# A fused attention and DeltaNet layer on one core: two head steps moved in a hand-written slot schedule

## What is computed

```python
bqkv = short_conv(bqkv, conv_w)                 # 4 taps back in time, then SiLU
g = -exp(a_log) * softplus(balpha + dt_bias);  beta = sigmoid(bbeta)
q = l2_normalize(q) * dk ** -0.5;  k = l2_normalize(k)
decay = exp(where(causal, g[i] - g[j], -inf))   # g summed up over the tokens
lower = where(strict, (k * beta) @ k.T * decay, 0)
tmat  = inverse(eye + lower)                    # unit lower triangular
...                                             # products with tmat, q and the state
o = rms_norm(o, dn_norm_gain) * silu(bz)
merged = sigmoid(gate_a) * (ya @ w_branch_a) + sigmoid(gate_b) * (yb @ w_branch_b)
out = rms_norm(x + merged @ w_out)
```

## Time and profile before

| what | value |
|---|---|
| median of 3 runs | 838.61 us (836.59 to 840.05) |
| the profiled execution, its own time | 838.09 us |
| its span, first to last instruction | 836.4 us |
| mean granted TensorE clock | 0.996 of full speed |
| busy: PE, PEld, DVE, ACT, POOL | 811.0, 665.5, 484.0, 411.0, 140.3 us |
| moved by DMA | 142.15 MB, 170 GB/s over the span |

### The profile page before, as it was taken

The page is one execution under the profiler, slowest core; times in us unless marked ns, Lnnn a source line. Parts: engine busy times, 40 slices in busy tenths (PEclk is TensorE's granted clock), DMA queues, the critical chain, the costliest instruction groups (busy, mean ns, idle before and its releaser), DMA issues.

```text
span 836.4 us, 12563 instructions
## 1 busy us (share of the span) xinstructions
PE 811.0 (97%) x3859; PEld 665.5 (80%) x3859; DVE 484.0 (58%) x794; ACT 411.0 (49%) x641; POOL 140.3 (17%) x222
## 2 busy tenths in 40 slices
PE   8899999999999999999999999999999999999996
PEld 7788877878787888778877878787788778888874
DVE  4676448545754664576448555754664466775562
ACT  4564545544544555454545544544555464444441
POOL 9112112110211021102112110211031100001120
PEclk9999999999999999999999999999999999999999
DMA  8855564565556455655565565556455565678652
GB/s 210 230 150 175 137 188 141 167 176 150 176 150 167 135 176 150 176 150 176 146 180 151 150 175 150 176 150 176 126 177 149 176 196 183 188 220 295 194 160 100
DMA packets 179207, 142.15 MB, mean 170 GB/s; under 512 B 10880, under 2 KB 144240, under 8 KB 179056
## 3 DMA queue, kind: packets, MB, share of 16 engines
q1 hardware_dynamic: 179184, 141.85, 58.4%
HBM read 139.72 MB, written 2.10 MB: 170 GB/s over the span
## 4 chain that ended last, share of the span: by engine, by line
PE 43%; issue 36%; POOL 8%; DVE 6%; ACT 3%; SPq 2%; DMA 1%; POOLq 0%; DVEq 0%; ACTq 0%
PE pj L498 12%; PE pj L496 12%; PE pj L497 12%; POOL xo L429 4%; POOL mt L427 3%; ACT w_hi L783 1%; PE dn_ps L551 1%; DVE w_lo L1008 1%; DVE conv L1118 1%; DVE decay L1105 1%; ACT L848 1%; SPq L268 1%; SPq L251 1%; POOL kn L423 1%; DVE conv L1115 1%
## 5 line engine op out<-in xcount | busy, mean ns | idle before, releaser
L1008 DVE TENSOR_TENSOR w_lo<-w_raw,w_hi 128x1024 fp32r<-128x1024 f32 x251 | 312.1, 1249 | 182.6 <-ACT w_hi L783 181.9
L496 PE MATMUL pj<-w_hi,xt_hi 128*128 128x512 f32 x860 | 357.1, 415 | 2.9 <-DVE w_lo L1008 2.8
L498 PE MATMUL pj<-w_hi,xt_lo 128*128 128x512 f32 x860 | 338.7, 394 | 0.0
L783 ACT ACTIVATE w_hi<-w_raw 128x1024 fp32r<-128x1024 f32 x251 | 264.6, 1059 | 149.7 <-PE pj L498 133.2
L497 PE MATMUL pj<-w_lo,xt_hi 128*128 128x512 f32 x860 | 336.4, 391 | 0.0
L498 PEld LDWEIGHTS pj<-w_hi,xt_lo 128*128 128x128 f32 x860 | 161.7, 188 | 36.6
L496 PEld LDWEIGHTS pj<-w_hi,xt_hi 128*128 128x128 f32 x860 | 162.6, 189 | 33.0 <-issue 3.5
L497 PEld LDWEIGHTS pj<-w_lo,xt_hi 128*128 128x128 f32 x860 | 162.9, 189 | 27.6
L429 POOL TENSOR_TENSOR xo<-v,own 128x128 f32<-128x128 f32 x48 | 44.6, 930 | 233.5 <-DVE v L1172 231.7
L872 ACT ACTIVATE ysb<-dn_ps 128x128 f32<-128x128 f32 x48 | 13.2, 276 | 63.0 <-PE dn_ps L568 63.0
L1172 DVE TENSOR_TENSOR v<-v,dn_ps 128x128 f32<-128x128 f32 x48 | 13.8, 287 | 45.5 <-PE dn_ps L573 44.6
(11 more groups left out here) (259 smaller groups left out, 784.0 us busy)
## 6 DMA issues: line engine op xcount, KB each, us to landing
w_raw<-in_w_in_dram SPq DMA_DIRECT2D x384, 256.0 KB, 3.1
w_raw<-in_w_out_dram SPq DMA_DIRECT2D x64, 256.0 KB, 3.7
w_raw<-in_w_branch_a_dram SPq DMA_DIRECT2D x32, 256.0 KB, 3.4
w_raw<-in_w_branch_b_dram SPq DMA_DIRECT2D x32, 256.0 KB, 3.6
gate<-in_x_dram SPq DMA_DIRECT2D x8, 256.0 KB, 5.5
gate<-in_x_dram SPq DMA_DIRECT2D x4, 512.0 KB, 7.5
gate<-in_final_norm_gain_dram SPq DMA_DIRECT2D x1, 1024.0 KB, 9.1
out_dram<-gate SPq DMA_DIRECT2D x1, 768.0 KB, 3.6
```

The lines of the kernel that those rows point to most:

```text
L496: pe.matmul(bank[:, t, :], hi[:, k, tok], w_hi[:, slot, cs], start=(k == 0), stop=False)
L498: mm = pe.matmul(bank[:, t, :], lo[:, k, tok], w_hi[:, slot, cs], start=False, stop=(k == kt_all - 1))
L783: act.activation(w_hi[:, slot, :], w_raw[:, slot, :], ACT.Copy).then_inc(hi_ready, 1)
L1008: dve.tensor_tensor(w_lo[:, slot, :], w_raw[:, slot, :], w_hi[:, slot, :].bitcast(F32), ALU.subtract).then_inc(lo_ready, 1)
```

## The change

It moves pieces between slots and cuts one wait in two.

- `S_Y0`, `S_R1`, `S_Y1`, `S_O` and `S_YT` stand two slots later (55, 57, 59, 61, 65).
- PE's L576 waits for the first mask of `xf` alone; the wait for the second stands ahead of L583.
- `S_DEC` is 16 in heads 1 to 7 and stays 20 in the first head. DVE's five decay blocks go with it, ahead of the convolution; the last two taps keep slot 20 (`S_CONV`). ACT's `Exp` follows in slot 17.
- ACT's SiLU goes from slot 23 to slot 22, where it stands ahead of the slot's weight copy.
- ACT's copy of the next head to `dn_nat` gets a wait for `o_squared`.

```diff
-S_TURN, S_DEC, S_KK = 18, 20, 24
+S_DEC, S_TURN, S_CONV, S_SILU, S_KK = 16, 18, 20, 22, 24
+S_DEC_FIRST = 20
-S_Y0, S_R1, S_Y1, S_O, S_YT = 53, 55, 57, 59, 63
+S_Y0, S_R1, S_Y1, S_O, S_YT = 55, 57, 59, 61, 65
...
-                if s == S_DEC:
+                if s == (S_DEC_FIRST if first else S_DEC):
                     pe.wait_ge(hs_ready, h + 1)
...
                 if s == S_Y0:
-                    pe.wait_ge(xf_ready, T * h + T)
+                    pe.wait_ge(xf_ready, T * h + 1)
...
                 if s == S_Y1:
                     pe.wait_ge(r1_ready, h + 1)
+                    pe.wait_ge(xf_ready, T * h + T)
...
                         act.wait_ge(dn_z_ready, h)
+                        act.wait_ge(o_squared, T * h)
...
-                if s == S_DEC + 1:
+                if s == (S_DEC_FIRST if first else S_DEC) + 1:
                     act.wait_ge(dsub_ready, 5 * (h + 1))
                     act.activation(decay[:, :, :], decay[:, :, :], ACT.Exp).then_inc(dexp_ready, 1)
-                if s == S_KK - 1:
+                if s == S_SILU:
                     act.wait_ge(conv_step, 12 * h + 12)
...
-                if s in (S_TURN, S_DEC):
+                if s == (S_DEC_FIRST if first else S_DEC):
+                    dve.wait_ge(dec_done, h + 1)
+                    if not first:
+                        dve.wait_ge(kk_ready, 3 * h)
...
+                                                 op0=ALU.subtract, op1=ALU.add).then_inc(dsub_ready, 1)
...
+                                          0.0, ALU.add, ALU.min).then_inc(dsub_ready, 1)
+                if s in (S_TURN, S_CONV):
...
                     for back in ((0, 1) if s == S_TURN else (2, 3)):
-                        if back == 2:
...
```

More of the change, by code:

```diff
@@ L1088, in dn_step @@
             def dn_step(s, h, first=False):
-                if s in (S_TURN, S_DEC):
+                if s == (S_DEC_FIRST if first else S_DEC):
+                    dve.wait_ge(dec_done, h + 1)
+                    if not first:
+                        dve.wait_ge(kk_ready, 3 * h)
+                    e1 = E[:, P:2 * P]
+                    e1_flip = E[:, 2 * P - 1:P - 1:-1]
+                    for block, t, e, mask in ((D00, 0, E[:, 0:P], later), (D11, 1, e1, later_flip),
+                                              (D11R, 1, e1_flip, earlier)):
+                        dve.scalar_tensor_tensor(out=decay[:, block, :], in0=e,
+                                                 scalar=hs[:, C_CUM + t:C_CUM + t + 1], in1=mask[:, :],
+                                                 op0=ALU.subtract, op1=ALU.add).then_inc(dsub_ready, 1)
+                    for block, e in ((D01, e1), (D01R, e1_flip)):
+                        dve.tensor_scalar(decay[:, block, :], e, hs[:, C_REST:C_REST + 1],
+                                          0.0, ALU.add, ALU.min).then_inc(dsub_ready, 1)
+                if s in (S_TURN, S_CONV):
                     if s == S_TURN:
```

## The result

The changed kernel takes **824.84 us** (median of 4 runs, 823.2 to 826.69), the kernel before 838.39 us in the same comparison (836.59 to 840.05). The ratio is 0.9843, 95% interval 0.9825 to 0.986. The profiled execution took 824.77 us, with a span of 823.1 us against 836.4. The forecast was 825.4 us, and 824.9 us for the profiled execution.

A forecast was written before the change was run, and what follows sets the result against it. PE's own work and the holes in it bound the kernel. Terms 8.9 + 5.7 + 0.8 - 2.2 = 13.2 us took the profiled 838.09 to 824.9; the median forecast was 825.4 us, range 821.5 to 831.0.

The forecast's parts named there:

- L577, two slots later: PE's wait for POOL's `xf`, 1.11 us a head, goes with the two-slot shift: gain 8.9 us.
- L552, `convs` in time: PE's wait for ACT's `convs` goes with the SiLU ahead of the weight copy: gain 5.7 us.
- L593 behind the loop: PE's single wait for `yb` behind the loop goes: gain 0.8 us, an estimate between 0 and 0.8.
- L539, new wait: PE's transposes of slot 18 wait for DVE's `yb_lo`, 0.32 us a head in 7 heads: -2.2 us.
- Reading the holes from start to start: On PE's timeline, a wait's loss exceeds its idle time: 1.11 us against 0.84, 0.72 against 0.47.
- The other count of a table load: On ACT, 1.38 us drain plus 1.28 us load; first head keeps its wait, sum 12.2 in place of 13.2.
- For PE that is worth about 0: Decay rows in slot 16 end DVE's convolution earlier, sparing 0.9 us, but gain PE about 0.
- a row of L538 that names `yb_lo`: Expected sign in PE's waits: 7 times, 0.1 us or less idle, some 0.3 to 0.5 us each on PEld.
- The bigger wait: Rival at PE's transposes of slot 18: each head gives back 1.45 us instead of 0.32, 833.3 us; chance 0.13.
- `hs` was copied 2.1 us before L547: Check at `S_DEC`: 2.0 us to spare; slower rival, `hs` late holds PE, 845.6 us at 5.2 late; chance 0.03.
- L497 waited for `w_lo`: Rival that the holes move: PE's weight stream can't follow, the gain is gone, 838 +- 4; chance 0.06.

The follow-up runs named there:

- Run 1: Kernel before with only the five later steps shifted by two slots, plus the cut wait: 828.03 us against 838.19.
- run 10: Changed kernel, but L577 waits for both masks again: 824.71 us against 837.14 for the kernel before.
- run 4: Kernel before, every step in its old slot, with only the wait cut so that L577 waits for the first mask: 834.48 us against 837.89.
- runs 2 and 3: Kernel before with the cut wait plus one move: the SiLU in slot 22 (829.66 us), or the decay rows in slot 16 (829.37 us), against 838.19.
- run 11: Changed kernel with the five steps one slot later than before in place of two: 822.48 us against 837.89 for the kernel before.
- run 5: Kernel before with only the SiLU moved to slot 22, the full wait for both masks kept: 833.0 us against 837.89.
- runs 3 and 7: First: kernel before with the decay rows' move and the cut wait, 829.37 us. Second: changed kernel with the SiLU back in slot 23, 825.43 us.
- run 6: Changed kernel without the decay rows' move, slot 20 in every head: 821.9 us against 838.19 for the kernel before.
- run 8: Changed kernel with DVE's split of slot 16 put in slot 17 behind `yb_lo`, in heads 1 to 7: 822.67 us against 837.14.
- run 9: Changed kernel with three more decay-like DVE instructions ahead of the five blocks in heads 1 to 7: 830.32 us against 837.14.
- Run 12: Kernel before, with DVE's split of slot 4 waiting for both of POOL's masks in heads 1 to 7: 831.3 us against 837.85.

## Why the prediction was right

The terms of the sum, each beside what the trace of the changed kernel shows:

| term | predicted | measured |
|---|---|---|
| L577, two slots later | 8.9 | 8 x (1.48 - 0.38) = 8.8 |
| L552, `convs` in time | 5.7 | 7 x 0.72 + 0.63 = 5.7 |
| L593 behind the loop | 0.8 | wait row gone; 1.14 to 0.37 us, 0.8 |
| L539, new wait | -2.2 | -7 x (1.14 - 0.80) = -2.4 |
| sum | 13.2 | 12.9; the span lost 13.3 |

The last two numbers differ in part by PE's wait at the start for the DMA of `x` (L482, now L483): 1.1 us before, 0.5 after. It is in no term of the sum and lies between 0.3 and 1.5 us in these traces. That 13.2 comes as near as 0.1 to 13.3 is so far luck; that each term is right to 0.2 us is not.

- **Reading the holes from start to start** carried the forecast. The idle times in the earlier trace rows add up to 10.9 us. The trace gave back 15.3, and then lost 2.4.
- **The shift.** Run 1, the shift without the other moves, gained 10.2 us where its two terms say 9.7. That the cut wait adds nothing to it is shown by run 10. What I had not priced is the cut without the shift: it is worth 3.4 us (run 4), which is why runs 2 and 3 came out below what I expected. And one slot would have been enough for the mask (run 11).
- **The SiLU.** The table load did begin ahead of the convolution's end, by 3.4 us. "This move alone takes away nearly all of the loss" holds: 4.9 us in run 5, where the trace leaves 0.06 us a head of the wait. The other count of a table load, by which the first head would have kept its wait (a sum of 12.2), is answered by the first head: the load ran from 55.08 to 56.36, the convolution ended at 56.62, the SiLU began at 56.65, and L552 started 0.23 us behind the last large matmul, as without a wait.
- **The decay rows.** "For PE that is worth about 0" holds beside the SiLU's move. What I had not said is that either of the two clears the wait of `convs` by itself (runs 3 and 7). So in the change one of them is spare: the rows' move in all heads, or the SiLU's in all but the first. Without the rows' move the time is 821.9 (run 6), and L539's steps are 2.1 us shorter in all. The prediction had both numbers, -2.2 for the new wait and about 0 for the rows, and didn't set them against each other.
- **The new wait.** DVE's blocks started 0.74 us behind L547, the split 1.30 later, `yb_lo` 1.13 later, all as forecast. PE started 3.73 us behind L547, not 3.64, since it needed 0.14 us behind `yb_lo`'s end, not 0.06; so it was 0.30 us late, not 0.21. The first product then cost 0.04 more, not 0.11 (and the two waits that I took this from say 0.10). Two small errors cancelled: 0.34 a head for 0.32. That DVE's order makes this wait is shown by runs 6, 8 and 11, which take it away but for 0.00 to 0.06 us in three different ways, and by run 9, which adds 0.78 us to its cause and finds no slack.
- **What I said of the views** was partly wrong. I expected a row of L538 that names `yb_lo`. PE's waits have none after the change, and PEld's put it down to issue, 0.5 us each. In runs 7 and 10, with the same order in DVE, PE's waits name it for one of the seven, 0.2 us.
- **A slip** in the range: 823.2 less 2.0 is 821.2, where I wrote 821.5. The result lies far from it.
- **The rivals.** The bigger wait didn't come: DVE's split of slot 14 ended 1.2 us before the blocks began, by DVE's idle time ahead of them. `hs` was copied 2.1 us before L547, against 2.0 forecast. L497 waited for `w_lo` 3.1 us in all, against 2.8.

## What to carry to other kernels

On an engine that is always "busy", read its holes from the start of one instruction to the start of the next and against a step of the same make that doesn't wait; here idle time showed 10.9 us of 15.3, and PE's waits had no row for the new one. When two moves aim at one wait, try each alone: one may be enough, and the other's price stays. A step that is moved later brings its results closer to whoever needs them: look up what stands ahead of the last of them on its engine, and put the short instruction that PE waits for ahead of the long one that nobody needs yet.

## What was unexpected

POOL's first mask took 1.37 us and the second 0.45, with the same shape, and I had taken this as given. Run 12 shows that DVE's split, running beside it, made the difference. In the trace before, the split ran from 183.43 to 184.65 us and the mask was issued at 183.59 and ended at 184.96, 0.31 us behind the split's end. With the split held back the mask took 0.46 us. It isn't this mask alone. POOL's L429, a product of `v` with another mask, has these times in the trace before:

```profile
L429 POOL TENSOR_TENSOR xo<-v,own x48: 460/917/1450, 64.8 to 648.4; 128x128 f32<-128x128 f32 x48
```

The median is a mixture: by the timeline 24 of the 48 began while a split ran and took 1.37 to 1.45 us, and the 24 others took 0.46 to 0.47.

The Trainium skill ("SBUF — State Buffer", Who interferes with whom) says that a VectorE instruction with two SBUF inputs contends with a GpSimd instruction that reads SBUF, for ports that only one of them can hold at a time. Here both read two operands from SBUF, and the trace agrees in the main: the mask ended only behind the split. But 0.31 us behind it is less than the 0.46 us that the mask takes by itself, so some 0.15 us of it passed beside the split; which part that is no run shows. The price of a split at the wrong moment was 0.9 us a head, four fifths of the 1.11 us of the wait that the change was made to step around.

On ScalarE, the kernel with only the decay rows moved has the table load from 209.78 to 211.06 us and the SiLU at 211.07. So the load cost its 1.28 us and no more in this order too.
